# A fourth expert body with a 32-slot base tile, own sums at each expert's end, and one jump to each larger body

## What is computed

```python
masked = jnp.where(in_group, aff_g, -1.0).reshape(-1, N_EXPERTS)
top_val, top_idx = lax.top_k(masked, TOP_K)
top_w = top_val / top_val.sum(-1, keepdims=True)
combine = jnp.sum(jax.nn.one_hot(top_idx, N_EXPERTS) * top_w[..., None], axis=1)
y = jnp.zeros_like(t)
for e in range(N_EXPERTS):
    hid = jax.nn.silu(t @ w_gate[e]) * (t @ w_up[e])
    y = y + combine[:, e:e + 1] * (hid @ w_down[e])
...
x = layer_norm(DEEPNORM_ALPHA * x + g2 * y, ln2_g[l], ln2_b[l])
```

## Time and profile before

| what | us |
|---|---|
| median of 3 runs | 1790.05 |
| lowest, highest | 1787.77, 1793.58 |
| the profiled execution | 1788.96 |
| its span, first to last instruction | 1787.1 |

### The profile page before, as it was taken

The page is one execution under the profiler, slowest core; times in us unless marked ns, Lnnn a source line. Parts: engine busy times, 40 slices in busy tenths (PEclk is TensorE's granted clock), DMA queues, the critical chain, the costliest instruction groups (busy, mean ns, idle before and its releaser), DMA issues.

```text
span 1787.1 us, 22339 instructions
## 1 busy us (share of the span) xinstructions
PE 1689.7 (95%) x9444; PEld 992.1 (56%) x9444; DVE 601.3 (34%) x1080; ACT 186.5 (10%) x440; POOL 361.4 (20%) x161
## 2 busy tenths in 40 slices
PE   7799999999999999989899999899999989899986
PEld 6578888888888878643344443333434224334322
DVE  0453657877667143331120311112111111111114
ACT  0001013110011100140100010100101001001001
POOL 0005730277777768200000000000000000000000
PEclk9899999999999999989999999999999999999998
DMA  9997895678877564359958899999999999899995
GB/s 385 423 427 209 352 399 229 277 316 348 341 312 326 244 267 176 123 237 429 424 246 349 361 402 426 426 386 426 424 427 427 427 428 427 367 425 424 428 427 205
DMA packets 51028, 630.10 MB, mean 353 GB/s; under 512 B 5775, under 2 KB 8240, under 8 KB 11848
## 3 DMA queue, kind: packets, MB, share of 16 engines
q1 hardware_dynamic: 49768, 623.15, 84.0%
q10 hardware_dynamic: 1120, 5.01, 0.7%
HBM read 624.47 MB, written 3.67 MB: 351 GB/s over the span
## 4 chain that ended last, share of the span: by engine, by line
PE 74%; DMA 18%; DVE 4%; issue 1%; POOL 1%; SPq 0%; ACT 0%; DVEq 0%; POOLq 0%; ACTq 0%
PE bank L1415 23%; PE bank L865 22%; PE bank L877 10%; PE bank L1177 8%; DMA ring<-in_w_up_gate 7%; DMA ring<-in_ada_w 4%; PE bank L836 3%; DMA region_g<-in_w_up_gate 3%; PE bank L889 3%; PE bank L1253 2%; DMA region_g<-in_w_down 2%; DMA ring<-in_w_down 2%; DVE ada_rows L1944 2%; DMA ring<-in_w_in 1%; POOL ring L736 1%
## 5 line engine op out<-in xcount | busy, mean ns | idle before, releaser
L865 PE MATMUL bank<-ring,region_b 128*64 128x512 f32 x1792 | 407.3, 603 | 33.2 <-DMA ring<-in_w_up_gate 31.3
L736 POOL TENSOR_TENSOR ring<-ring 128x1024 f32<-128x1024 f32 x152 | 359.0, 2389 | 331.5 <-DMA ring<-in_w_in 224.6
L865 PEld LDWEIGHTS bank<-ring,region_b 128*64 128x64 f32 x1792 | 124.5, 138 | 287.6 <-issue 253.3
L877 PE MATMUL bank<-ring,region_f 128*64 128x512 f32 (+1 forms) x1312 | 225.6, 528 | 6.7 <-DMA ring<-in_w_down 6.7
L1415 PE MATMUL bank<-ring,region_a 128*128 128x256 f32 x768 | 171.3, 380 | 0.5 <-ACT region_g L1739 0.5
L1415 PE MATMUL bank<-ring,region_x 128*128 128x256 f32 x768 | 170.4, 379 | 0.9 <-issue 0.7
L1415 PEld LDWEIGHTS bank<-ring,region_a 128*128 128x128 f32 x768 | 145.3, 190 | 23.0 <-issue 2.7
L1415 PEld LDWEIGHTS bank<-ring,region_x 128*128 128x128 f32 x768 | 145.3, 190 | 21.1 <-issue 1.1
L877 PEld LDWEIGHTS bank<-ring,region_f 128*64 128x64 f32 (+1 forms) x1312 | 74.4, 128 | 140.4 <-issue 117.9
L1944 DVE SCALAR_TENSOR_TENSOR bank<-ring,condT,bank 128x512 f32<-128x512 f32 x192 | 144.8, 754 | 5.8
L2378 DVE TENSOR_TENSOR region_a<-bank,region_a 128x512 f32<-128x512 f32 x128 | 79.7, 683 | 179.3 <-PE bank L889 179.0
(11 more groups left out here) (235 smaller groups left out, 1314.6 us busy)
## 6 DMA issues: line engine op xcount, KB each, us to landing
ring<-in_w_up_gate SPq DMA_DIRECT2D x112, 2048.0 KB, 19.3
ring<-in_w_down SPq DMA_DIRECT2D x56, 2048.0 KB, 16.1
ring<-in_ada_w SPq DMA_DIRECT2D x44, 2048.0 KB, 11.9
ring<-in_w_in SPq DMA_DIRECT2D x31, 2048.0 KB, 13.8
region_g<-in_w_up_gate SPq DMA_DIRECT2D x16, 2048.0 KB, 18.3
ring<-in_w_branch SPq DMA_DIRECT2D x8, 2048.0 KB, 14.5
ring<-in_w_out SPq DMA_DIRECT2D x8, 2048.0 KB, 9.9
region_g<-in_w_down SPq DMA_DIRECT2D x8, 2048.0 KB, 23.3
```

What stands on the lines that cost most here:

```text
L736: ins = pool.tensor_tensor(quarter(s, *out)[:, k:k + 4, :], quarter(s, *in0)[:, k:k + 4, :], quarter(s, *in1)[:, k:k + 4, :], op)
L865: last = nc.tensor.matmul(bank_of(x, j)[n * c:n * c + n, 0:2 * m], tokens(x, 8 * half + k), w[:, k % 4, :, m * c:m * c + m], start=(half = ...
L877: last = nc.tensor.matmul(bank_of(x, q)[n * c:n * c + n, 0:m], hidT[x][:, k, :], w[:, k % 4, m * c:m * c + m], start=(k == 0), stop=(k == ...
```

## The change

1. A further body, `NARROW`: for up to 32 tokens the base tile has 32 slots and runs like an extra tile, in four column strips of 256 columns. It stands in line. The 64-slot body without extra tiles (`wide`) now stands behind the program.
2. Each expert adds its own results: `add_up(q)` moves from the next expert's body to the end of its own. In bodies without extra tiles the first sum stands before the wait for the last half.
3. The branches are a chain of four compares, and each leads directly to its body. On PE three of them are announced, in the narrow body only.
4. DVE makes the weights of the token choice (`hotw`) in the body, no longer ahead of the branch.

```diff
+WIDE, NARROW = 0, 5
+NARROW_SLOTS = 32
+CLASSES = ((EXTRA[3][0], "all_extra", (1, 2, 3, 4)), (EXTRA[2][0], "two_extra", (1, 2)), (CAP, "one_extra", (1,)),
+           (NARROW_SLOTS, "wide", ()))
...
             here = nc.cur_bb
-            jump = eng.br_cond(count > EXTRA[1][0], on_true=f"{name}_more", on_false=f"{name}_few")
-            if announced is not None:
-                jump.branch_hint(announced)
-            nc.switch_bb(f"{name}_few", parent=here)
-            body(())
+            for n, (most, kind, xs) in enumerate(CLASSES):
+                jump = eng.br_cond(count > most, on_true=f"{name}_{kind}", on_false=f"{name}_up_to_{most}")
+                if announced is not None and n > 0:
+                    jump.branch_hint(announced[n - 1])
+                nc.switch_bb(f"{name}_up_to_{most}", parent=here)
+            body(None)
...
+        def announce(pe, ne):
+            large_announced[ne] = [pe.mark_branch_hint_location() for _ in CLASSES[1:]]
...
+            for most, kind, xs in reversed(CLASSES):
+                more = nc.body(f"{name}_{kind}", parent=here, valid_engines=[engine])
+                with more:
+                    announced = eng.mark_branch_hint_location() if engine in announcing else None
+                    body(xs)
+                    eng.sem_inc(extra_end[engine], 1)
+                    leave(eng, f"{name}_end", announced)
...
-            def add_up(of, q):
-                pe.wait_ge(y_ready, (g * GRP + of) * 2 + 3 + q)
+            def add_up(q):
+                pe.wait_ge(y_ready, ne * 2 + 3 + q)
                 if q == 0:
-                    pe.wait_ge(extras_added, g * GRP + of + 1)
-                for a in range(TT):
-                    for c in range(2):
-                        b = 2 * a + c
-                        pe.wait_ge(m_taken[b], add_job(g, of, q, last_turn) + 1)
-                        scatter(psum[SUM_BANKS[b]][:, :], back0[of % 2], 0, ysb[q], c, a).then_inc(m_full[b], 1)
+                    pe.wait_ge(extras_added, ne + 1)
+                for b in range(len(SUM_BANKS)):
+                    pe.wait_ge(m_taken[b], add_job(g, le, q, last_turn) + 1)
+                    if base == WIDE:
+                        last = scatter(psum[SUM_BANKS[b]][:, :], back0[le % 2], base, ysb[q], b % 2, b // 2)
+                    else:
+                        for a in range(TT):
+                            last = scatter(psum[SUM_BANKS[b]][:, a * 256:(a + 1) * 256], back0[le % 2], base,
+                                           ysb[q][:, 0:256], b, a)
+                    last.then_inc(m_full[b], 1)
...
-            def sums_amid_base():
-                gate_up(0, 0, 0, range(2))
-                if le > 0:
-                    add_up(le - 1, 0)
-                gate_up(0, 0, 0, range(2, 5))
-                if le > 0:
-                    add_up(le - 1, 1)
-                gate_up(0, 0, 0, range(5, 8))
+            def base_ahead():
+                gate_up(0, 0, 0)
...
-            if not xs and ne < NE - 1:
-                large_announced[ne + 1] = pe.mark_branch_hint_location()
-            down(0, 1, first).then_inc(half_used, 1)
+            if base == NARROW and ne < NE - 1:
+                announce(pe, ne + 1)
+            down(base, 1, first).then_inc(half_used, 1)
             if 0 < len(xs) < 3:
                 extra("add F")(1)
+            if not xs:
+                add_up(0)
             loaded_half(5, 1)
-            early = le == GRP - 1 and not xs
-            if early:
-                add_up(le, 0)
-            down(0, 1, last).then_inc(y_full, 1)
+            down(base, 1, last).then_inc(y_full, 1)
             if len(xs) == 2:
                 extra("add F")(2)
-            if le == GRP - 1:
-                if not early:
-                    add_up(le, 0)
-                add_up(le, 1)
+            if xs:
+                add_up(0)
+            add_up(1)
```

142 lines of the change are left out of this document (62 added, 80 removed).

## The result

The changed kernel took 1797.3 us (median of 11, 1793.1 to 1801.7) against 1787.8 us for the kernel before (median of 11, 1785.3 to 1793.6): a ratio of 1.0052, 95% interval 1.0043 to 1.0061. I had said 1788.1, between 1779 and 1797. Its first profiled execution took 1793.15 us with a span of 1791.4, 4.3 above the span of before. From median to median the change costs 9.5 us. So two things need a cause: the 4.3 us of the profiled executions, where I had -1.9, and some 4 us more in the median of the changed kernel, which that execution does not hold. (The last 1.2 us lie in the kernel before, whose profiled execution, 1788.96, was that much above its own median.)

A forecast was written before the change was run, and what follows sets the result against it. Bound: the DMA stream plus the holes three large experts tear into it. Balance -1.5 through expert 5's entry, code +2.9, tail -3.3 sum to -1.9 us on a span of 1787.1; applied to the median 1790.05: 1788.1, range 1779 to 1797.

The follow-up runs named there:

- wide_ahead: The changed kernel, but each body with one extra tile also announces its successor's wide jump, so expert 1 announces the jump to expert 5; 1805.5 us.
- no_narrow: The changed kernel without its narrow body, the 64-slot body in line for all experts with up to 64 tokens; 1791.5 us, 1.0023 of the kernel before.

## What to carry to other kernels

Where a stream of data is full except for holes, work moved out of a hole and set directly behind it is not moved off the path: ask of every moved step what the engine's successor needs next, and do it for every place of that kind, not for the largest alone. A cheaper path for most cases sends the rest over a costlier one; price the rest first, and try it at single places. Where an engine waits and then has work in the path, look at the clock of that work. And profile a kernel more than once when its times spread more than those of before.

## What the runs showed that I had not expected

- Of two or three branch announcements in a row on PE's sequencer only the first was served: 0.37 to 3.1 us for its jump, 5.9 to 7.2 for the others. With one made later (wide_ahead), an earlier one whose jump was still to come did not serve (6.06 us for it, against 0.32).
- A branch announced alone was not always ready: 0.3 to 3.7 us, once 6.35, and 0.8 to 3.7 for the same one in six executions of one kernel.
- Jumps that were not announced, or whose announcement was lost, took 5.9 to 7.3 us, with one instruction packet (q8) in the 6.00 us of the changed kernel's jump into expert 1 and two in the 7.25 us of the unannounced one before. This was paid only where the data was there first: 7.88 us idle ahead of expert 5, while expert 1 began at 1159.06 us with a jump of 6.00 us and at 1158.94 with one of 0.37.
- The granted clock fell in the narrow stretches to 0.84 on average without a change in the rate of data; at 1.00, by added work, the kernel took 1800.2 us and so gained nothing.
- After 2.71 us idle behind expert 0 the sums ran at the low clock in the changed kernel (6.15 us) and at the full one in no_narrow (4.89 us). Why the one and not the other stays open.
- A MATMUL instruction of 128x512 with 128 columns of weights took 0.44 us; those with 64 columns, two side by side, came to 0.227 us each.
